# Eight slices of a modulation product multiplied and summed on VectorE instead of TensorE, with two short TensorE sums

## The chip, the core and the metric

The kernel runs on one core of a Trainium2 chip. The metric is the device time of one execution in microseconds. TensorE is called PE in the profile, VectorE DVE, ScalarE ACT, GpSimd POOL, and SyncE, which issues nearly all transfers here, SP.

## The reference, cut to what matters

The program is one layer of a hybrid backbone over 256 context and 1024 sample tokens with 1024 channels. Each of two conditioning vectors (`c_ctx` for the context tokens, `c` for the samples) gives six rows of 1024 numbers that shift, scale and gate the layer:

```python
def modulation(cond, w_ada, b_ada):
    m = jax.nn.silu(cond) @ w_ada + b_ada        # (1, 1024) @ (1024, 6144)
    return jnp.split(m[:, None, :], 6, axis=-1)   # sh1, sc1, g1, sh2, sc2, g2

h = adaln(xp, norm_mix[l], sh1, sc1)              # needed before the projection
... = project(h, ...)                             # h @ w_in, 1024 x 2848
xp = xp + g1 * merge(...)                         # g1: after the mixer
h = adaln(xp, norm_ff[l], sh2, sc2)
xp = xp + g2 * sq_relu_mlp(h, w_ff1[l], w_ff2[l])
```

Only sh1 and sc1 are needed before the projection. The other four rows, g1, sh2, sc2 and g2, are needed by later stages.

## The kernel before

**The projection stage.** `project` multiplies the normalised tokens by `w_in` in ten groups of 256 or 304 columns (`GROUPS`). A group is a row of items: ten items (one for each tile of 128 tokens) in groups 0 to 2 and 7 to 9, six items (two blocks of 128 channels by three chunks of tokens) in groups 3 to 6. `ITEMS` numbers them 0 to 83: group 1 is items 10 to 19, group 2 is 20 to 29, group 3 is 30 to 35, group 4 is 36 to 41 and group 5 begins at 42. An item is 24 matmuls (8 channel tiles, each as high*high, high*low and low*high part), written by `token_item` or `channel_item` into one of four PSUM banks; `acc_ready` counts them. All engines run through the same list of item numbers in their own programs, and each does at number `n` what the tables of numbers give it there. Each engine works strictly in the order of its program.

**What each engine does at an item.** ACT or DVE copies item `n` out of PSUM (`evacuate`; `on_act(n)` says who), and TensorE waits for that before item `n + 4`. SP stores it. Before group `g + 1` ACT splits the group's weights into a high part (L820) and POOL makes the low part (`split`, L876), which TensorE waits for at the group's first item (`wlo_ready`). SP loads the weights of a group into one of two rooms, `raw[:, 0]` and `raw[:, 1]`, in turn.

**The gates.** Beside the items runs another chain. SP loads 32 columns of the projection back (L541, in SP's program at item 12). TensorE turns them in three pieces (`Gates.pe_turn`, L572, behind items 15, 17 and 19); piece 0 waits for the load, and piece 1 and 2 each wait for `lrT_ready` of the piece before, which DVE raises with `dve_turned` (L584, at items 15, 17 and 19). DVE also makes a low part of the gate weights at item 14 (L563). From item 20 on, every seventh item has three matmuls of gate logits (L594), worked up by ACT and then by DVE in four steps (L619, L625, L631, L639 to L650).

**The modulation.** `w_ada` is used in three parts of 2048 columns; a slice is 128 of its 1024 rows by those 2048 columns, 1 MB. The first part (sh1, sc1) is done before the projection. The other sixteen slices are spread over the items of groups 2 to 9 (`slices`, `slice_at`). SP loads a slice into the room whose weights have just been split (`sp_later`, L154) and TensorE multiplies it (`pe_slice`, L198):

```python
for j in range(4):
    mm = pe.matmul(bank[32 * j:32 * j + 32, :], self.silu[:, k, :], src[:, j * HALF:(j + 1) * HALF], start=(k == 0), stop=(k == KD - 1))
```

Each of the four matmuls has the 32 columns of `silu` (two of them in use, one for each conditioning vector) as stationary operand and 512 moving columns, and writes its own 32 rows of a PSUM bank. After eight slices DVE adds the bias (`dve_rows`, L216), TensorE turns the rows into columns (`pe_turn`, L221) and DVE picks what is needed (`dve_pick`). The slices of part 1 stand behind items 23, 27, 32, 35, 38, 41, 44 and 47, those of part 2 behind items 53 to 78.

Of the kernel before, what the change touches and what calls it, by code (L numbers as in the profile page):

```python
# [20 lines left out]
P = 128  # L21
# [87 lines left out]
class Modulation:  # L109
# [5 lines left out]
    def __init__(self, s, keep, a, scratch, raw, mod_out):  # L115
# [3 lines left out]
        self.gain = s.sb("ada_gain", [P, 2, KD])  # L119
        self.gain_rows = s.sb("ada_gain_rows", [2 * KD, P])  # L120
# [22 lines left out]

    def sp_cond(self, sp):
# [7 lines left out]

    def sp_later(self, sp, m, k, j):
        sp.dma_start(self.raw_slice(j), self.source(m, k)).then_inc(self.later_in[j], 16)  # L154

    def bias(self, eng, m):
        if m:
            eng.wait_ge(self.cols_ready, m)
            if m == 2:
                eng.wait_ge(self.mod_out, 32)  # L160
        else:
            eng.wait_ge(self.cleared, 2)
        for j in range(4):
            at = (4 * m + j) * HALF
            eng.dma_start(self.rows[32 * j:32 * j + 2, :], self.a["b_ada"][:, at:at + HALF].broadcast_to([2, HALF])).then_inc(self.bias_in, 16)

# [12 lines left out]
    def dve_silu(self, dve):  # L179
        dve.memset(self.rows[:, :], 0.0).then_inc(self.cleared, 1)  # L180
        dve.memset(self.silu[:, :, :], 0.0).then_inc(self.cleared, 1)
        dve.wait_ge(self.e_ready, 1)
# [24 lines left out]
    def pe_later(self, pe, bank, m, k, j, count):  # L207
        if k == 0 and m > 1:
            pe.wait_ge(self.shift_ready, m)
        pe.wait_ge(self.later_in[j], 16 * count)  # L210
        self.pe_slice(pe, bank, self.raw_slice(j), k)

    def dve_rows(self, dve, bank, m):
        dve.wait_ge(self.slice_used, KD * (m + 1))
        dve.wait_ge(self.bias_in, 16 * 4 * (m + 1))
# [8 lines left out]
    def dve_pick(self, dve, bank, m):  # L224

        cols = bank.rearrange("p (b j r) -> p j b r", j=4, r=32)[:, :, :, 0:2]
        where = {0: ((0, 0, 0), (1, 0, 2)), 1: ((0, 1, 2),), 2: ((1, 1, 0),)}[m]
# [13 lines left out]
    def sp_store(self, sp, m):  # L241

        sp.wait_ge(self.rows_ready, m + 1)
        for j in ((0, 1) if m == 1 else (2, 3)):
# [408 lines left out]
def project(nc, keep, a, raw, hi, lo, scratch, outs, keys, rec, room, stored, mod_out):  # L653
# [4 lines left out]
    with ExitStack() as ctx:  # L658
# [26 lines left out]
        slices = [(g, at) for g, places in ((2, (3, 7)), (3, (2, 5)), (4, (2, 5)), (5, (2, 5)), (6, (5,)), (7, (2, 5, 9)), (8, (1, 5, 9)), (9, (4,))) for at in places]  # L685
        slice_at = {FIRST_ITEM[g] + at: i for i, (g, at) in enumerate(slices)}
        slice_load_at = {}
        for i, (g, at) in enumerate(slices):
            same = i and slices[i - 1][0] == g
            slice_load_at[FIRST_ITEM[g] + (slices[i - 1][1] + 1 if same else 0 if g < 7 else -1 if g == 7 else -3)] = i  # L690
        used_until = [sum(1 for g, at in slices if g <= f) for f in range(NG)]
        slice_count = [sum(1 for g, at in slices[:i + 1] if g % 2 == slices[i][0] % 2) for i in range(len(slices))]
        BANK = ps[:, 7]
        rows_at = {FIRST_ITEM[6]: 1, FIRST_ITEM[9] + 5: 2}
        cols_at = {FIRST_ITEM[6] + 1: 1, FIRST_ITEM[9] + 6: 2}
        pick_at = {FIRST_ITEM[6] + 2: 1, FIRST_ITEM[9] + 7: 2}
        assert len(slices) == 2 * KD and slices[KD - 1][0] == 5 and slices[KD] == (6, 5)

        def on_act(n):

            return n < NT or n % 2 == 1
# [19 lines left out]
        with nc.Block() as block:  # L721

            @block.sync
            def _(sp):
# [31 lines left out]
                for n in range(LAST):  # L756
# [3 lines left out]
                    if n == FIRST_ITEM[g] and 1 <= g < NG - 1:  # L760
# [4 lines left out]
                        if used_until[g - 1]:  # L765
                            sp.wait_ge(ada.slice_used, KD + used_until[g - 1])
                        load_group(sp, a, raw, g + 1, (g + 1) % 2).then_inc(w_in[(g + 1) % 2], 16)
                    if n in slice_load_at:
                        i = slice_load_at[n]
                        room = slices[i][0]  # L770
                        sp.wait_ge(wlo_ready, room)
                        sp.wait_ge(ada.slice_used, KD + (i if room == g else used_until[room - 2]))
                        ada.sp_later(sp, 1 + i // KD, i % KD, room % 2)
                    store(n)
                    if n == NT:
# [3 lines left out]
                        ada.bias(sp, 1)  # L779
# [7 lines left out]
                    if n - 1 in pick_at:  # L787
                        ada.sp_store(sp, pick_at[n - 1])
# [2546 lines left out]
```

## Time and profile before

| | |
|---|---|
| time, median of 3 runs | 1642.98 us (1642.93 to 1643.2) |
| the profiled execution, its own time | 1642.75 us |
| span of its instructions | 1641.0 us |
| PE busy | 1587.1 us (97%) |
| DVE, POOL, ACT busy | 977.2, 1018.1, 687.4 us |
| projection stage on PE, from item 10 to the end | about 83 to 388 us |

The span runs from the first to the last instruction; the execution's own time is 1.8 us more. A busy share counts instructions under way, so the share of an engine says where it has idle time and not how well it works. Times of rows are microseconds from the span's start.

### The profile page before, as it was taken

To read this page: it belongs to the slowest core of one execution; us is meant where nothing else is said; L and a number is where in the kernel's file an instruction comes from. 1 tells how busy PE (TensorE), PEld (TensorE's weight loads), DVE (VectorE), ACT (ScalarE), POOL (GpSimd) and SP (SyncE) were. 2 spreads that over 40 slices of the span, in tenths; PEclk is the share of its full clock that TensorE was granted. 3 is DMA by queue.
4 is the path that set the end of the run, shared out by engine and by line. 5 is a ranking of instruction groups with operands and counts; after the bars stand their busy time and mean duration, and the time that the engine had idled before them with its cause. 6 is when DMAs were issued, how large, how long until landed. Compare 5 with 4: busy or idle time off the path is not lost.

```text
span 1641.0 us, 31942 instructions
## 1 busy us (share of the span) xinstructions
PE 1587.1 (97%) x11619; PEld 1388.8 (85%) x11619; DVE 977.2 (60%) x1503; ACT 687.4 (42%) x1213; POOL 1018.1 (62%) x784
## 2 busy tenths in 40 slices
PE   5999999998999999999899999999999999999998
PEld 1998778997788877788789899898979899998987
DVE  2733564775665575347865756666684545545468
ACT  2513323324454666213444444444545444444441
POOL 1711455573585899004687778677898767677673
PEclk9999999999999999999999999999999999999999
DMA  9254655749745654334643132231344132231313
GB/s 345 89 146 151 199 177 192 259 141 248 225 161 178 213 175 136 132 133 154 209 164 103 51 102 77 76 102 51 103 140 143 52 102 79 75 102 51 102 52 116
DMA packets 209402, 225.93 MB, mean 138 GB/s; under 512 B 50688, under 2 KB 169616, under 8 KB 206096
## 3 DMA queue, kind: packets, MB, share of 16 engines
q1 hardware_dynamic: 209248, 224.46, 43.1%
q8 instruction: 70, 1.15, 0.3%
q14 instruction: 36, 0.29, 0.1%
q10 hardware_dynamic: 48, 0.02, 0.0%
HBM read 177.22 MB, written 47.24 MB: 137 GB/s over the span
## 4 chain that ended last, share of the span: by engine, by line
PE 44%; POOL 4%; DVE 1%; issue 1%; DMA 0%; ACT 0%; SPq 0%; DVEq 0%; ACTq 0%; POOLq 0%
PE ff_banks L3200 8%; PE ff_banks L3201 8%; PE ff_banks L3202 8%; PE ff_banks L3173 7%; PE ff_banks L3175 7%; PE ff_banks L3174 7%; POOL h_whi L2846 1%; POOL h_xop L2443 1%; POOL h_wlo L2858 1%; POOL h_whi L2853 1%; DVE ff_tmp L3047 0%; DMA ff_hb<-in_w_ff 0%; DVE ff_acc L3037 0%; PE ff_banks L3215 0%; PE ff_banks L3216 0%
## 5 line engine op out<-in xcount | busy, mean ns | idle before, releaser
L3173 PE MATMUL ff_banks<-h_xop,h_whi 128*128 128x320 f32 x888 | 275.2, 310 | 4.6 <-POOL h_whi L2846 2.0
L3175 PE MATMUL ff_banks<-h_xop,h_whi 128*128 128x320 f32 x888 | 274.4, 309 | 0.0
L3174 PE MATMUL ff_banks<-h_xop,h_whi 128*128 128x320 f32 x888 | 274.3, 309 | 0.0
L3004 DVE TENSOR_TENSOR ff_acc<-ff_acc,ff_banks 128x512 f32<-128x512 f32 x296 | 200.4, 681 | 100.7 <-PE ff_banks L3202 99.1
L3200 PE MATMUL ff_banks<-h_wlo 128*128 128x512 f32 x580 | 226.5, 390 | 1.6 <-POOL h_whi L2853 0.8
L3202 PE MATMUL ff_banks<-h_wlo 128*128 128x512 f32 x580 | 225.6, 389 | 0.0
L2846 POOL TENSOR_TENSOR h_whi<-mid_raw,h_whi 128x512 fp32r<-128x512 f32 x149 | 208.5, 1415 | 1.4 <-ACT h_whi L2698 1.4
L2858 POOL TENSOR_TENSOR h_wlo<-mid_raw,h_wlo 128x320 fp32r<-128x320 f32 x128 | 116.8, 914 | 127.3 <-ACT mid_raw L2735 127.3
L3173 PEld LDWEIGHTS ff_banks<-h_xop,h_whi 128*128 128x128 f32 x888 | 166.7, 188 | 8.3 <-issue 3.6
L3174 PEld LDWEIGHTS ff_banks<-h_xop,h_whi 128*128 128x128 f32 x888 | 166.7, 188 | 1.1
L3175 PEld LDWEIGHTS ff_banks<-h_xop,h_whi 128*128 128x128 f32 x888 | 166.7, 188 | 0.0
L981 PE MATMUL prj_banks<-prj_whi,h_hi 128*128 128x304 f32 x480 | 147.6, 308 | 5.1 <-POOL h_lo L351 2.9
L2846 POOL TENSOR_TENSOR h_whi<-ff_tmp,h_whi 128x512 fp32r<-128x512 f32 x63 | 105.6, 1676 | 67.7 <-ACT h_whi L2698 67.7
L983 PE MATMUL prj_banks<-prj_whi,h_lo 128*128 128x304 f32 x480 | 144.9, 302 | 0.0
L982 PE MATMUL prj_banks<-prj_wlo,h_hi 128*128 128x304 f32 x480 | 144.3, 301 | 0.0
L2698 ACT ACTIVATE h_whi<-mid_raw 128x512 fp32r<-128x512 f32 x149 | 90.0, 623 | 97.7 <-DVE mid_raw L2960 91.4
L3200 PEld LDWEIGHTS ff_banks<-h_wlo 128*128 128x128 f32 x580 | 108.9, 188 | 25.0 <-DVE ff_acc L3004 1.9
L3202 PEld LDWEIGHTS ff_banks<-h_wlo 128*128 128x128 f32 x580 | 108.9, 188 | 22.9
L2728 ACT ACTIVATE mid_raw<-wo_raw 128x320 f32<-128x320 f32 x128 | 60.3, 471 | 159.4 <-DVE wo_raw L2982 65.2
L3201 PE MATMUL ff_banks<-h_whi,h_wlo 128*128 128x512 f32 x310 | 120.7, 390 | 0.0
L831 ACT ACTIVATE prj_stage<-prj_banks 128x304 f32<-128x304 f32 (+2 forms) x47 | 21.0, 447 | 221.2 <-PE prj_banks L983 134.4
L3201 PE MATMUL ff_banks<-h_wlo 128*128 128x512 f32 x290 | 113.1, 390 | 0.0
(326 smaller groups left out, 3771.2 us busy)
## 6 DMA issues: line engine op xcount, KB each, us to landing
mid_raw<-in_w_ff SPq DMA_DIRECT2D x124, 512.0 KB, 4.4
mid_raw<-in_w_ada SPq DMA_DIRECT2D x18, 1024.0 KB, 7.0
early_room<-qk_by_channel SPq DMA_DIRECT2D x20, 512.0 KB, 4.1
proj<-prj_stage SPq DMA_DIRECT2D x60, 152.0 KB, 1.9
mid_raw<-in_w_in SPq DMA_DIRECT2D x6, 1216.0 KB, 7.7
early_room<-in_w_ada SPq DMA_DIRECT2D x6, 1024.0 KB, 10.4
decays<-early_room SPq DMA_DIRECT2D x8, 640.0 KB, 4.5
early_room<-decays SPq DMA_DIRECT2D x20, 256.0 KB, 2.8
```

The lines of the kernel that those rows point to most:

```text
L981: pe.matmul(out, x_hi, whi[j][:, k, 0:w], start=(k == 0), stop=False)
L982: pe.matmul(out, x_hi, wlo[j][:, k, 0:w], start=False, stop=False)
L983: mm = pe.matmul(out, x_lo, whi[j][:, k, 0:w], start=False, stop=(k == KD - 1))
L2846: pool.tensor_tensor(lo, source(q, i), hi.bitcast(F32), ALU.subtract).then_inc(w1lo_ready, 1)
L2858: pool.tensor_tensor(ulo[j][c][:, t0:t0 + TH], v[i % 2], uhi[j][c][:, t0:t0 + TH].bitcast(F32), ALU.subtract).then_inc(ulo_ready, 1)
L3004: dve.tensor_tensor(acc[:, p, at], acc[:, p, at], down[n % RING], ALU.add).then_inc(added, 1)
L3173: pe.matmul(out, w_hi[:, k], x_hi[:, k], start=(k == 0), stop=False)
L3174: pe.matmul(out, w_hi[:, k], x_lo[:, k], start=False, stop=False)
L3175: mm = pe.matmul(out, w_lo[:, k], x_hi[:, k], start=False, stop=(k == KH - 1))
L3200: pe.matmul(out, x_hi, w_hi[c][:, at], start=(c == 0), stop=False)
L3201: pe.matmul(out, x_hi, w_lo[c][:, at], start=False, stop=False)
L3202: mm = pe.matmul(out, x_lo, w_hi[c][:, at], start=False, stop=(c == 1))
```

## The change

The eight slices of part 1 (g1 and sh2) leave TensorE. They are loaded in another cut: 256 rows of `w_ada` by 1024 columns, again 1 MB, first the four loads of g1 (`u = 0`) and then the four of sh2 (`u = 1`). DVE multiplies each row by its number of `silu` and adds up over the channel tiles in `sums`, four instructions of 128x1024 for each load. What then is left, the sum over the 128 partitions, TensorE makes with four matmuls for each `u`, whose stationary operand `pick` is a column of ones (`pe_sum`). The loads begin in group 1 instead of group 2. The bias rows, the stores of g1 and the turn of sh2 move with it, and ACT evacuates all items below 36, where DVE took the even ones from 10 on. A parameter of the build makes a reserved piece of on-chip memory smaller; `sums` is a new tensor there.

```diff
+    def sp_early(self, sp, i, j):
+        u, q = i // 4, i % 4
+        src = self.a["w_ada"][0, 2 * q * P:(2 * q + 2) * P, self.quarter(u):self.quarter(u) + 2 * HALF]
+        sp.dma_start(self.raw_slice(j).rearrange("p (k n) -> p k n", k=2), src.rearrange("(k p) n -> p k n", p=P)).then_inc(self.later_in[j], 16)
...
+    def dve_early(self, dve, i, k, j, count):
+        u, q = i // 4, i % 4
+        dve.wait_ge(self.later_in[j], 16 * count)
+        for c in range(2):
+            t = 4 * i + 2 * k + c
+            by = self.silu[:, 2 * q + k, c:c + 1]
+            in_ = self.raw_slice(j)[:, 2 * k * HALF:(2 * k + 2) * HALF]
+            if t % 16 < 2:
+                if u:
+                    dve.wait_ge(self.sum_ready, u)
+                op = dve.tensor_scalar(self.sums[:, c], in_, by, None, ALU.mult)
+            else:
+                dve.wait_ge(self.product_ready, t - 1)
+                op = dve.scalar_tensor_tensor(self.sums[:, c], in_, by, self.sums[:, c], ALU.mult, ALU.add)
+            op.then_inc(self.product_ready, 1)
+
+    def pe_sum(self, pe, bank, u):
+        pe.wait_ge(self.picked, 3)
+        pe.wait_ge(self.product_ready, 16 * (u + 1))
+        if u:
+            pe.wait_ge(self.rows_ready, u + 1)
+        for c, j, row, at in self.places(u):
+            mm = pe.matmul(bank[row - c:row - c + 32, :], self.pick[:, c], self.sums[:, c, j * HALF:(j + 1) * HALF], start=True, stop=True)
+        mm.then_inc(self.sum_ready, 1)
...
-        slices = [(g, at) for g, places in ((2, (3, 7)), (3, (2, 5)), (4, (2, 5)), (5, (2, 5)), (6, (5,)), (7, (2, 5, 9)), (8, (1, 5, 9)), (9, (4,))) for at in places]
+        early = ((1, 0, 1, 1), (1, 2, 3, 3), (1, 4, 5, 5), (2, 0, 1, 2), (2, 3, 4, 5), (2, 6, 7, 8), (3, 0, 1, 2), (3, 3, 4, 5))
+        late = ((6, 5), (7, 2), (7, 5), (7, 9), (8, 1), (8, 5), (8, 9), (9, 4))
...
+        sum_at = {FIRST_ITEM[2] + 4: 0, FIRST_ITEM[4] + 1: 1}
+        early_rows_at = {n + 1: u for n, u in sum_at.items()}
+        shift_turn, shift_at = FIRST_ITEM[4] + 3, FIRST_ITEM[4] + 4
...
-            return n < NT or n % 2 == 1
+            return n < FIRST_ITEM[4] or n % 2 == 1
...
+                    if n in early_load_at:
+                        i = early_load_at[n]
+                        room = early[i][0]
+                        sp.wait_ge(wlo_ready, room)
+                        before = i if i and early[i - 1][0] == room else early_until[room - 2] if room > 1 else 0
+                        if before:
+                            sp.wait_ge(ada.product_ready, 4 * before)
+                        ada.sp_early(sp, i, room % 2)
...
-    nc = bacc.Bacc("TRN2", target_bir_lowering=False, num_devices=1)
+    nc = bacc.Bacc("TRN2", target_bir_lowering=False, num_devices=1, dynamic_dma_scratch_size=1024)
```

An entry of `early` is the group whose room is used, the item of that group at which SP loads, and the two items at which DVE multiplies the first and the second half. The loads are called 0 to 7 below.

On DVE, group 1 read before, from the first copy out of PSUM to the third piece of the turned columns:

```order
L913 COPY prj_stage<-prj_banks 128x304 x2
L563 TENSOR_TENSOR prj_wgk<-early_room,prj_wgk 32x1024
L584 TENSOR_TENSOR prj_lrT<-prj_banks,prj_lrT 32x512
L913 COPY prj_stage<-prj_banks 128x304
L584 TENSOR_TENSOR prj_lrT<-prj_banks,prj_lrT 32x512
L913 COPY prj_stage<-prj_banks 128x304
L584 TENSOR_TENSOR prj_lrT<-prj_banks,prj_lrT 32x256
```

and now, in the changed kernel's line numbers (L634 is L563 of before, L655 is L584):

```order
L250 TENSOR_SCALAR prj_ada_sums<-mid_raw,prj_ada_silu 128x1024 x2
L253 SCALAR_TENSOR_TENSOR prj_ada_sums<-mid_raw,prj_ada_silu,prj_ada_sums 128x1024 x6
L634 TENSOR_TENSOR prj_wgk<-early_room,prj_wgk 32x1024
L655 TENSOR_TENSOR prj_lrT<-prj_banks,prj_lrT 32x512
L253 SCALAR_TENSOR_TENSOR prj_ada_sums<-mid_raw,prj_ada_silu,prj_ada_sums 128x1024 x4
L655 TENSOR_TENSOR prj_lrT<-prj_banks,prj_lrT 32x512
L655 TENSOR_TENSOR prj_lrT<-prj_banks,prj_lrT 32x256
```

Eight products now stand ahead of the gate weights and piece 0, and four more between piece 0 and piece 1; the copies are gone to ACT.

On SP, the same stretch read before, from the gate weights' bias to the weights of group 3:

```order
L165 DMA prj_ada_rows<-in_b_ada 2x512 x4
L735 DMA proj<-prj_stage 128x304 x2
L541 DMA early_room<-proj 128x10x32 x3
L735 DMA proj<-prj_stage 128x304 x7
L387 DMA mid_raw<-in_w_in 128x8x256
```

and now (L812 is the store of an item, L612 the load of the gates' columns, L458 the load of a group's weights, L167 one of the new loads):

```order
L187 DMA prj_ada_rows<-in_b_ada 1x512 x4
L812 DMA proj<-prj_stage 128x304
L167 DMA mid_raw<-in_w_ada 128x2x1024
L812 DMA proj<-prj_stage 128x304
L612 DMA early_room<-proj 128x10x32 x3
L812 DMA proj<-prj_stage 128x304
L167 DMA mid_raw<-in_w_ada 128x2x1024
L812 DMA proj<-prj_stage 128x304 x6
L458 DMA mid_raw<-in_w_in 128x8x256
```

Loads 1 and 2 have moved into this stretch (load 0 stands further ahead, at item 10), and load 1 stands in front of the gates' columns. All three use room 1, so each waits until the products of the one before are done.

## Rows read from the trace of the kernel before

**Rows 1.** The page: busy time and share of each engine.

```profile
PE 1587.1 (97%) x11619; PEld 1388.8 (85%) x11619; DVE 977.2 (60%) x1503; ACT 687.4 (42%) x1213; POOL 1018.1 (62%) x784
```

**Rows 2.** Busy time by stretch: PE, PEld, DVE, ACT, POOL, clock, DMA share, GB/s.

```profile
83.00:388.00 305.00, 303.24 (x1940) 269.29 (x1938) 158.79 (x170) 88.47 (x106) 125.56 (x78) 1.00 0.59 187
```

**Rows 3.** Waits of PE from 83 to 388: total, times, longest.

```profile
PE prj_banks L198 <- DMA mid_raw<-in_w_ada: 0.5, 1, 0.5
```

**Rows 4.** Timeline, items 23 to 25 leaving PSUM, a slice behind 23.

```profile
130.56 0.42 ACT L831 ACTIVATE prj_stage<-prj_banks 128x304 f32<-128x304 f32 x1 [0.84 <-PE prj_banks L983]
135.08 0.47 DVE L913 COPY prj_stage<-prj_banks 128x304 f32<-128x304 f32 x1 [5.55 <-PE prj_banks L983]
138.42 0.43 ACT L831 ACTIVATE prj_stage<-prj_banks 128x304 f32<-128x304 f32 x1 [5.63 <-PE prj_banks L983]
```

**Rows 5.** DVE line 296: ns min/median/max.

```profile
L296 DVE TENSOR_SCALAR head_x<-head_x,head_rstd x10: 735/753/1645, 24.8 to 66.2; 128x1024 f32<-128x1024 f32 x10
```

**Rows 6.** DVE by form: total and mean ns of one.

```profile
L1409 DVE TENSOR_TENSOR early_at<-mix_gla,keep_mats 128x1024 f32<-128x1024 f32 x20 | 24.4, 1221 | 2.1 <-PE mix_gla L1297 1.5
L488 DVE SCALAR_TENSOR_TENSOR prj_xn<-early_room,prj_rstd 128x640 f32<-128x640 f32 x10 | 8.2, 816 | 1.8 <-POOL prj_rstd L462 1.8
```

**Rows 7.** Timeline of SP's queue, group 1.

```profile
82.94 0.43 SPq L387 DMA_DIRECT2D mid_raw<-in_w_in  x1
...
93.52 0.83 SPq L735 DMA_DIRECT2D proj<-prj_stage  x2
94.53 2.08 SPq L541 DMA_DIRECT2D early_room<-proj  x3
```

**Rows 8.** Landing of the slice issued at 117.76, behind a group's weights.

```profile
DMA to landing us min/median/max: 7.8/7.8/7.8
```

**Rows 9.** Landing of the slice issued at 131.65, alone.

```profile
DMA to landing us min/median/max: 5.2/5.2/5.2
```

**Rows 10.** Landing of the gates' columns, L541, three loads.

```profile
DMA to landing us min/median/max: 2.7/3.8/3.9
```

**Rows 11.** Timeline of PE, turned pieces 0, 1, 2 of the gates.

```profile
101.96 0.60 PE L572 MATMUL prj_banks<-keep_mats,early_room 128*96 128x128 f32 x4
...
109.09 0.60 PE L572 MATMUL prj_banks<-keep_mats,early_room 128*96 128x128 f32 x4
...
116.20 0.38 PE L572 MATMUL prj_banks<-keep_mats,early_room 128*96 128x128 f32 x2
```

**Rows 12.** Timeline of POOL and DVE, group 1.

```profile
99.05 5.41 POOL L876 TENSOR_TENSOR prj_wlo<-mid_raw,prj_whi 128x2432 fp32r<-128x2432 f32 x1 [17.94 <-ACT prj_whi L820]
...
99.33 6.21 DVE L563 TENSOR_TENSOR prj_wgk<-early_room,prj_wgk 32x1024 fp32r<-32x1024 f32 x1
```

**Rows 13.** Timeline of DVE, pieces 0 and 1.

```profile
105.57 0.68 DVE L584 TENSOR_TENSOR prj_lrT<-prj_banks,prj_lrT 32x512 fp32r<-32x512 f32 x1
...
110.35 0.68 DVE L584 TENSOR_TENSOR prj_lrT<-prj_banks,prj_lrT 32x512 fp32r<-32x512 f32 x1 [3.59 <-ACT prj_lrT L578]
```

**Rows 14.** Timeline of DVE, POOL and ACT, group 4.

```profile
195.97 1.91 ACT L820 ACTIVATE prj_whi<-mid_raw 128x2048 fp32r<-128x2048 f32 x1
...
198.28 0.42 DVE L911 TENSOR_SCALAR prj_stage<-prj_banks 128x256 f32<-128x256 f32 x1 [5.24 <-PE prj_banks L993]
...
207.89 4.61 POOL L876 TENSOR_TENSOR prj_wlo<-mid_raw,prj_whi 128x2048 fp32r<-128x2048 f32 x1
```

**Rows 15.** Timeline of PE, end of group 4 (item 41).

```profile
213.20 0.75 PE L594 MATMUL prj_banks<-prj_lrT,prj_wgk 96*128 96x512 f32 x3
213.88 1.07 PE L198 MATMUL prj_banks<-mid_raw,prj_ada_silu 128*32 128x512 f32 x8
```

**Rows 16.** Timeline of PE and DVE, rows of part 1.

```profile
251.57 0.68 DVE L216 TENSOR_TENSOR prj_ada_rows<-prj_banks,prj_ada_rows 128x512 f32<-128x512 f32 x1
...
256.89 0.60 PE L221 MATMUL prj_banks<-keep_mats,prj_ada_rows 128*128 128x128 f32 x4
```

**Rows 17.** Landing of all sixteen slices, L154.

```profile
DMA to landing us min/median/max: 5.1/6.7/10.0
```

More of the change, by code:

```diff
@@ new lines, in pe_sum, with dve_early_rows @@
+    def pe_sum(self, pe, bank, u):
+        pe.wait_ge(self.picked, 3)
+        pe.wait_ge(self.product_ready, 16 * (u + 1))
+        if u:
+            pe.wait_ge(self.rows_ready, u + 1)
+        for c, j, row, at in self.places(u):
+            mm = pe.matmul(bank[row - c:row - c + 32, :], self.pick[:, c], self.sums[:, c, j * HALF:(j + 1) * HALF], start=True, stop=True)
+        mm.then_inc(self.sum_ready, 1)
+    def dve_early_rows(self, dve, bank, u):
+        dve.wait_ge(self.sum_ready, u + 1)
+        dve.wait_ge(self.bias_in, 16 * 4 * (u + 2))
+        dve.tensor_tensor(self.rows[:, :], bank, self.rows[:, :], ALU.add).then_inc(self.rows_ready, 1)
@@ new lines, in dve_shift, with sp_early_store @@
+    def dve_shift(self, dve, bank):
+        cols = bank.rearrange("p (b j r) -> p j b r", j=4, r=32)
+        dve.wait_ge(self.cols_ready, 2)
+        for c in range(2):
+            dve.tensor_copy(self.keep["shift"][:, 1].rearrange("p (j b) c -> p j b c", j=2)[:, :, :, c], cols[:, 2 * c:2 * c + 2, :, c]
+                            ).then_inc(self.shift_ready, 1)
+    def sp_early_store(self, sp):
+        sp.wait_ge(self.rows_ready, 2)
+        for c, j, row, at in self.places(0):
+            sp.dma_start(self.scratch["mod"][c:c + 1, at:at + HALF], self.rows[row:row + 1, :]).then_inc(self.mod_out, 16)
@@ new lines, in project @@
+        late = ((6, 5), (7, 2), (7, 5), (7, 9), (8, 1), (8, 5), (8, 9), (9, 4))
+        early_load_at = {FIRST_ITEM[g] + load: i for i, (g, load, a0, a1) in enumerate(early)}
+        early_at = [(FIRST_ITEM[g] + at, i, k) for i, (g, load, a0, a1) in enumerate(early) for k, at in enumerate((a0, a1))]
+        slice_at = {FIRST_ITEM[g] + at: i for i, (g, at) in enumerate(late)}
+        slice_load_at = {}
+        for i, (g, at) in enumerate(late):
+            same = i and late[i - 1][0] == g
+            slice_load_at[FIRST_ITEM[g] + (late[i - 1][1] + 1 if same else 0 if g < 7 else -1 if g == 7 else -3)] = i
@@ new lines, in project @@
+        early_until = [sum(1 for e in early if e[0] <= f) for f in range(NG)]
+        late_until = [sum(1 for e in late if e[0] <= f) for f in range(NG)]
+        slices = [e[0] for e in early + late]
+        slice_count = [sum(1 for g in slices[:i + 1] if g % 2 == slices[i] % 2) for i in range(len(slices))]
+        BANK = ps[:, 7]
+        sum_at = {FIRST_ITEM[2] + 4: 0, FIRST_ITEM[4] + 1: 1}
+        early_rows_at = {n + 1: u for n, u in sum_at.items()}
+        shift_turn, shift_at = FIRST_ITEM[4] + 3, FIRST_ITEM[4] + 4
@@ L699, in on_act @@
+        rows_at, cols_at, pick_at = FIRST_ITEM[9] + 5, FIRST_ITEM[9] + 6, FIRST_ITEM[9] + 7
+        assert len(early) == KD and len(late) == KD
         def on_act(n):
-            return n < NT or n % 2 == 1
+            return n < FIRST_ITEM[4] or n % 2 == 1
         def staged_value(n):
```

101 lines of the change are left out of this document (61 added, 40 removed).

## The prediction

> **What bounds the kernel now.** I read the page first: TensorE is busy 97% of the span, the other engines 42 to 62% [rows 1]. The reader sees that work taken from TensorE can shorten the kernel, and that the others have room on the average. The change lies in the projection stage, so I read its stretch next. TensorE is busy 303.24 of 305 us there, DVE 158.79, POOL 125.56, ACT 88.47, at full clock and with transfers at 0.59 of their time [rows 2]. Last I read what TensorE waits for there: one wait of 0.5 us, for a slice [rows 3]. So in this stage each microsecond of matmuls taken away counts in full, until TensorE starts to wait for something that today is ready just in time. The task is to find that.
>
> **What leaves TensorE.** Item 24 leaves PSUM 4.52 us after item 23, with a slice between them, and item 25 leaves 3.34 us after 24, without one [rows 4]. A slice thus costs 1.18 us of TensorE. Eight are removed, -9.4 us. Two sums of four matmuls are added; they have the shape of a slice (128 rows deep, 32 stationary and 512 moving columns), so I price them the same, +2.4. The turn of sh2 moves from item 49 to 39 and costs what it did. Net -7.1 us if nothing waits.
>
> **What DVE gets.** 32 instructions of 128x1024 in fp32. The four that open a sum scale one tensor, as line 296 does, 0.75 us [rows 5]. The other 28 have two tensors. A 128x1024 with one input in PSUM takes 1.22, and the same operation on 640 columns takes 0.82, of which 384 further columns at the same pace make 1.22 too [rows 6]. Some of it overlaps, so four take about 4.7. Together some 36 us over 100 us in which DVE is half idle, and it gives the copies of 13 items to ACT, which has the most room. The work fits; what counts is when each piece is done, because DVE, SP and TensorE take their programs in order.
>
> **The chain of loads in group 1.** Loads 0, 1 and 2 use one room, so each waits for the products of the one before.
> Load 0 is issued behind the weights of group 2, at 83.4 [rows 7]. A slice issued so landed after 7.8 us [rows 8]: 91.2. Two single and two double products, 3.9: 95.1.
> Load 1 is issued at 95.1. SP would have come there at about 94.2, so the store of item 12 and the gates' columns are issued some 1.6 us later than today's 94.53 [rows 7]. Load 1 alone takes 5.2 [rows 9]: 100.3.
> **Piece 0.** Today the gates' columns are issued by 96.6, the last landing 3.9 after its start near 95.7 [rows 7, 10], 99.6, and TensorE wants them at 101.96 [rows 11]: 2.4 to spare. Now they are 1.6 later and behind 1 MB, for which the queued slice paid 7.8 - 5.2 = 2.6 [rows 8, 9]. They land at 103.8, and TensorE waits 1.8.
> **Pieces 1 and 2.** When load 1 lands at 100.3, POOL is in its low part of group 2's weights, 99.05 to 104.46, and the DVE instruction with two on-chip inputs that began beside it took 6.21 us for what alone is some 1.2: it ended 1.08 after POOL did [rows 12]. I take the products to wait likewise (the nearest row; there is none of exactly this operation beside POOL). Then load 1's products run 104.5 to 109.2; the gate weights (1.2) and piece 0 (0.68, [rows 13]) make 111.1, 2 us after piece 1 is wanted at 109.09 [rows 11]. Load 2 is issued at 109.2, lands at 114.4, its products end at 119.1, and piece 1 of DVE, which stands behind them, at 119.8. TensorE wants it for piece 2 at 116.20 [rows 11]: 3.6 late, with hand-overs 4.0. The three waits are one delay after another on the same engine, so the largest counts, not the sum: +4.0.
> The bounds of this term: if the products don't wait for POOL, load 1's end at 105.0, load 2's at 114.9 and piece 1 at 115.6, in time; then piece 0's 1.8 is left. If also the columns land in time, 0. If load 2 lands after 7.8 instead of 5.2, +6.6.
>
> The Trainium skill, in "SBUF — State Buffer", section "Who interferes with whom", says that a VectorE instruction with two SBUF inputs and a GpSimd instruction that reads SBUF exclude each other for the whole instruction. It speaks of tensor_tensor. The trace agrees for that operation [rows 12]; for the three-operand product no run here shows it. By the rule the sum is the one above; without it 2.2 us less.
>
> **After group 1.** The chain goes on at about 12 us a load (issue to landing 5.2 to 7.8, products 4.7). Load 3 is issued with group 3's weights when load 2's products end, lands near 127, and its products end near 132. The first sum stands behind item 24, which leaves PSUM at 135.08 - 1.18 + 4.0 = 137.9 [rows 4]. Loads 4 to 7 then end near 146, 157, 171 and 187, also held back by gate work, by POOL's low parts and by the wait of SP for its item. The second sum stands behind item 37, some 3 us before item 38's 198.28 [rows 14]. So the sums have 5 to 8 us to spare. The group weights that now wait for products are tightest for group 5: issued at 187, landed by 193, and ACT splits them at 195.97 today [rows 14]. Under that cover all this costs nothing; without it each microsecond is one of TensorE's.
> **Group 5's weights.** Today POOL's low part for group 5 ends at 212.50, 14.2 after DVE copied item 38 at 198.28 [rows 14]. Between them stands a chain that starts with that copy. DVE now also adds the bias of the second sum there, 0.68 [rows 16]: 14.9. TensorE ends item 41 at 213.20 [rows 15], 14.9 after; less a slice (1.18), plus the turn (0.60 busy, some 0.4 of time, [rows 16]) and the gate logits (0.68, [rows 15]) it wants the weights at 14.8. The two are level: +0.2, bounds 0 and 1. Today's slack of 2.4 us (the slice at 213.88 takes about 1, [rows 15]) is gone, and what is later on DVE in group 4 is late on TensorE.
> Behind group 5 nothing is added to DVE, and the splits of groups 6 to 9 follow the copies of items, which come earlier with TensorE. The mixer's loads are issued behind the last items and move with them.
>
> **The sum.** -7.1 + 4.0 + 0.2 = -2.9 us. The profiled execution took 1642.75, so 1639.9; the median of the runs is 0.23 above it: 1640.1.
>
> **The rivals.**
> A, forecast: TensorE gains 7.1 and waits 3 to 5 us in group 1; -1.9 to -4.1, 1638.9 to 1641.1. Chance 0.55.
> B, the wait is small: the products pass POOL, or the columns and load 2 land early. For it speaks that no row shows this operation waiting; against it, that its nearest kin does [rows 12]. -4.9 with the wait for piece 0, -7.1 with none: 1635.9 to 1638.1. Chance 0.22.
> C, longer: transfers of the new cut land after 6.5 to 7.8, or POOL starts late behind weights that load 0 pushed back (it delays the gates' weights by up to 2.6, and ACT splits group 2 behind them). Then piece 1 is 6 to 8 late: net -1 to +1, 1642 to 1644. Chance 0.13.
> D, slower: slices of today land after up to 10.0 us [rows 17]. At 10.0 each of seven later loads is 4.8 behind my chain. Load 2 alone makes the wait 8.8, net +1.9. From where the five loads behind it add more than the 5 to 8 us to spare, the second sum waits as well, 5 x 4.8 = 24 less the 8 and less what TensorE has been held up already (9): +7 on top, +9, 1652. It decides from some 1.5 us a load. Against it: in today's order only stores of items stand in the queue between the gates' columns and group 3's weights, and the slice that was alone took 5.2 [rows 9]. Chance 0.10.
>
> **How the numbers follow.** A measurement of this kernel tells 0.2%, 3.3 us, from no change: faster is under 1639.7, slower over 1646.3. B is all faster, and of A about 0.35 of its 0.55, since its middle lies 0.4 us above the line: faster 0.22 + 0.21 = 0.43 with C adding none. D is slower for the larger part, 0.09, and C near none. Same is the rest, 0.48. The range takes A, most of B and C: 1636.0 to 1644.0, which leaves out D and a tenth besides. A's own range is 1638.9 to 1641.1.
>
> **What would show it.** In the profile after: slices behind eight items fewer and two sums; TensorE waiting for DVE line 655 (the third turned piece) 3 to 5 us near 116 to 120, and for the gates' columns near 102; a product of load 1 with a duration of about 5 us beside POOL's low part; no wait at the two sums; group 5's first matmul within a microsecond of POOL's end. The prediction is wrong if TensorE doesn't wait near 120, if it waits at a sum, or if the stage is shorter but the mixer gives it back, which would be seen as longer idle of TensorE behind its start.

## The result, and the profile after

The changed kernel takes 1649.03 us (median of 10 runs, 1646.59 to 1654.32), the one before 1643.15 (10 runs, 1642.64 to 1644.43): a ratio of 1.0038 (1.003 to 1.0046). It is 5.9 us slower where 2.9 faster was forecast. The profiled execution took 1649.0, and its page reads

```profile
span 1647.2 us, 31905 instructions
...
PE 1584.2 (96%) x11571; PEld 1391.1 (84%) x11571; DVE 1009.9 (61%) x1527; ACT 693.4 (42%) x1226; POOL 1017.1 (62%) x784
```

TensorE has 48 matmuls less (eight slices fewer and two sums more, each shown as x8) and is busy 2.9 us less [rows 1], yet the span is 6.2 us longer: its idle time has grown by 9. The view of waits, PE from 60 to 395 us (in total, times, longest), says at whose hands:

```profile
PE prj_banks L643 <- DVE prj_lrT L655: 4.5, 2, 2.8
PE prj_banks L643 <- DMA early_room<-proj: 2.6, 1, 2.6
PE mix_st L1597 <- PEq L95: 2.3, 1, 2.3
PE prj_banks L224 <- DMA mid_raw<-in_w_ada: 1.3, 1, 1.3
PE prj_banks L1089 <- POOL prj_wlo L967: 0.9, 1, 0.9
```

L643 is the turning of the gates' columns (L572 before), L655 the DVE step behind each piece, L224 a slice that stayed, L1089 the first matmul of group 5. Before, the stage had only the slice's wait, at 0.5 [rows 3]. The third row is at the start of the mixer, the stage behind the projection; the kernel before has 2.2 us there as well. The timeline of PE, all three turned pieces:

```profile
103.23 0.64 PE L643 MATMUL prj_banks<-keep_mats,early_room 128*96 128x128 f32 x4 [2.58 <-DMA early_room<-proj]
...
112.19 0.64 PE L643 MATMUL prj_banks<-keep_mats,early_room 128*96 128x128 f32 x4 [1.62 <-DVE prj_lrT L655]
...
122.36 0.67 PE L643 MATMUL prj_banks<-keep_mats,early_room 128*96 128x128 f32 x2 [2.85 <-DVE prj_lrT L655]
```

They stood at 101.96, 109.09 and 116.20 without a wait [rows 11]. Who made DVE late is in its timeline and POOL's:

```profile
90.21 1.42 DVE L250 TENSOR_SCALAR prj_ada_sums<-mid_raw,prj_ada_silu 128x1024 f32<-128x1024 f32 x2 [10.59 <-DMA mid_raw<-in_w_ada]
91.54 2.48 DVE L253 SCALAR_TENSOR_TENSOR prj_ada_sums<-mid_raw,prj_ada_silu,prj_ada_sums 128x1024 f32<-128x1024 f32 x2
100.10 10.07 DVE L253 SCALAR_TENSOR_TENSOR prj_ada_sums<-mid_raw,prj_ada_silu,prj_ada_sums 128x1024 f32<-128x1024 f32 x4 [6.09 <-DMA mid_raw<-in_w_ada]
110.20 1.22 DVE L634 TENSOR_TENSOR prj_wgk<-early_room,prj_wgk 32x1024 fp32r<-32x1024 f32 x1
111.45 0.68 DVE L655 TENSOR_TENSOR prj_lrT<-prj_banks,prj_lrT 32x512 fp32r<-32x512 f32 x1
116.72 4.87 DVE L253 SCALAR_TENSOR_TENSOR prj_ada_sums<-mid_raw,prj_ada_silu,prj_ada_sums 128x1024 f32<-128x1024 f32 x4 [4.58 <-DMA mid_raw<-in_w_ada]
121.62 0.68 DVE L655 TENSOR_TENSOR prj_lrT<-prj_banks,prj_lrT 32x512 fp32r<-32x512 f32 x1
```

```profile
100.14 5.36 POOL L967 TENSOR_TENSOR prj_wlo<-mid_raw,prj_whi 128x2432 fp32r<-128x2432 f32 x1 [20.47 <-ACT prj_whi L911]
```

Four products take 4.87 alone (load 2's, at 116.72) and 10.07 beside POOL's 5.36 (load 1's): 5.2 us more, about the length of POOL's instruction. The gates' columns are late in SP's queue:

```profile
94.10 0.39 SPq L167 DMA_DIRECT2D mid_raw<-in_w_ada  x1
94.54 1.04 SPq L812 DMA_DIRECT2D proj<-prj_stage  x1
95.75 4.93 SPq L612 DMA_DIRECT2D early_room<-proj  x3
...
110.24 0.37 SPq L167 DMA_DIRECT2D mid_raw<-in_w_ada  x1
```

The three loads of the columns (L612) start 1.2 us later than L541 did and take 4.93 us to issue instead of 2.08 [rows 7]. Last, what the waits did to the clock. The windows view (PE, PEld, DVE, ACT, POOL, clock, DMA share, GB/s) of an undisturbed stretch, of the third wait and of what follows it:

```profile
103.20:106.60 3.40, 3.37 (x25) 3.37 (x26) 3.40 (x2) 0.60 (x1) 2.30 (x1) 1.00 0.00 0
120.00:122.30 2.30, 0.00 (x0) 0.00 (x0) 2.27 (x3) 0.00 (x0) 0.00 (x0) 1.00 0.20 68
122.30:125.70 3.40, 3.34 (x14) 3.33 (x15) 0.42 (x2) 0.38 (x1) 0.00 (x0) 0.50 0.83 257
```

For 3.4 us behind the wait TensorE ran at 1.2 GHz instead of 2.4 and began 14 matmuls, not 25: 11 of 0.14 us, 1.5 us lost.

**Where the time went, by stretch.** I measure with the copies of items out of PSUM. Before, items 9, 20 and 83:

```profile
82.12 0.42 ACT L831 ACTIVATE prj_stage<-prj_banks 128x304 f32<-128x304 f32 x1 [2.91 <-PE prj_banks L983]
...
119.96 0.47 DVE L913 COPY prj_stage<-prj_banks 128x304 f32<-128x304 f32 x1 [2.41 <-PE prj_banks L983]
...
386.73 0.42 ACT L831 ACTIVATE prj_stage<-prj_banks 128x304 f32<-128x304 f32 x1 [4.54 <-PE prj_banks L983]
```

and in the changed kernel:

```profile
80.65 0.42 ACT L922 ACTIVATE prj_stage<-prj_banks 128x304 f32<-128x304 f32 x1 [2.91 <-PE prj_banks L1081]
...
127.68 0.42 ACT L922 ACTIVATE prj_stage<-prj_banks 128x304 f32<-128x304 f32 x1 [4.24 <-PE prj_banks L1081]
...
389.32 0.42 ACT L922 ACTIVATE prj_stage<-prj_banks 128x304 f32<-128x304 f32 x1 [4.54 <-PE prj_banks L1081]
```

Up to item 9 the changed kernel is 1.5 us ahead. The start differs from profile to profile (six of the twelve below are ahead by 1.3 to 1.6 us, the others by 0.1 to 0.5), and nothing of the change stands there. Item 9 to 20 takes 47.03 instead of 37.84, +9.2. Item 9 to 83, "the stage" from here on, takes 308.67 instead of 304.61: +4.1, where -2.9 was forecast. From there to the end it loses another 3.7.

### The profile page after: what moved, and what is told of

Same layout as the page of the kernel before. It is cut to its first block, busy times and chain, and to the rows that moved or that the text cites. A ratio compares the mean times of both kernels' runs of the same rounds, so it can differ in the third digit from the quotient of the medians.

```text
span 1647.2 us, 31905 instructions
## 1 busy us (share of the span) xinstructions
PE 1584.2 (96%) x11571; PEld 1391.1 (84%) x11571; DVE 1009.9 (61%) x1527; ACT 693.4 (42%) x1226; POOL 1017.1 (62%) x784
## 4 chain that ended last, share of the span: by engine, by line
PE 44%; POOL 4%; DVE 1%; issue 1%; DMA 0%; ACT 0%; DVEq 0%; POOLq 0%; ACTq 0%; SPq 0%
PE ff_banks L3302 8%; PE ff_banks L3303 8%; PE ff_banks L3304 8%; PE ff_banks L3275 7%; PE ff_banks L3276 7%; PE ff_banks L3277 7%; POOL h_whi L2948 1%; POOL h_xop L2545 1%; POOL h_wlo L2960 1%; POOL h_whi L2955 1%; DVE ff_tmp L3149 0%; DMA ff_hb<-in_w_ff 0%; POOL h_wlo L2955 0%; DVE ff_acc L3139 0%; DVE ff_acc L3106 0%
## 5 line engine op out<-in xcount | busy, mean ns | idle before, releaser
L922 ACT ACTIVATE prj_stage<-prj_banks 128x304 f32<-128x304 f32 (+2 forms) x60 | 26.8, 446 | 206.2 <-PE prj_banks L1081 128.8
```

## The experiments

All in one table first: the stage of each profile against before's 304.61 us, the median, and the ratio to the kernel before on record, with its 95% interval. The ratio is taken to executions of the kernel before that were timed beside the run (their medians lie between 1642.7 and 1643.7 us), and it isn't the quotient of two medians. The stage comes from one profiled execution of each kernel. For e3 and e12 that execution took 4.4 and 5.3 us more than the kernel's median (1648.08 and 1651.27), so their stages are likely longer than usual; for the others that were timed it lies within 2 us of the median.

| kernel | stage, us | median, us | ratio to before |
|---|---|---|---|
| the change | +4.1 | 1649.03 | 1.0038 (1.003 to 1.0046) |
| e1_memory | +0.3 | 1641.94 | 1.0003 (0.9994 to 1.0012) |
| e2_copies | 0.0 | 1643.64 | 1.0001 (0.9992 to 1.001) |
| e3_pool_later | +1.5 | 1643.64 | 1.001 (0.9999 to 1.002) |
| e4_order | +0.9 | 1645.32 | 1.0014 (1.0004 to 1.0023) |
| e5_tiny | +0.1 | 1643.02 | 0.9998 (0.9989 to 1.0008) |
| e6_order_all | +4.5 | 1650.05 | 1.004 (1.0026 to 1.0053) |
| e7_order_sum | +8.1 | 1653.85 | 1.0065 (1.0051 to 1.0079) |
| e8_seven_gone | -5.5 | 1636.8 | 0.9963 (0.9949 to 0.9976) |
| e9_both | -2.5 | 1644.01 | 1.0006 (0.9997 to 1.0016) |
| e10_semaphores | 0.0 | one profile | |
| e11_load_behind | +2.4 | one profile | |
| e12_group3 | +0.8 | 1645.95 | 1.0022 (1.0012 to 1.0033) |

The theory: the slices are worth what was said, and the chain load, product, shared room, next load is what makes TensorE wait in group 1. The rivals: the smaller reserved memory and the new tensors, the copies that went to ACT, or a gain that the mixer gives back.

**e1_memory** is the kernel before with the build parameter and the two new tensors, unused.

```diff
+        self.sums = s.sb("ada_sums", [P, 2, 2 * HALF])
+        self.pick = s.sb("ada_pick", [P, 2, 32])
...
+    nc = bacc.Bacc("TRN2", target_bir_lowering=False, num_devices=1, dynamic_dma_scratch_size=1024)
```

> The kernel before with only the smaller reserve of on-chip memory and the two new tensors allocated, not used. Chain theory (the time was lost in the projection stage, by waits of TensorE on DVE in group 1 and what follows): same as before, within 0.5 us. Layout theory (of the 6 us, the 3.7 that the profile after shows behind the projection stage come from other memory addresses): 2 to 4 us slower than before, all of it behind 390 us.

**e2_copies** adds to it that ACT copies all items below 36.

```diff
-            return n < NT or n % 2 == 1
+            return n < FIRST_ITEM[4] or n % 2 == 1
```

> As the first, and ACT copies all items below 36 out of PSUM, where DVE took the even ones. No load, product or slice is moved. Chain theory: same as before, within 1 us, as ACT is half idle and TensorE needs an item's bank only three items later. Copies theory (ACT behind gate work and behind stores is what TensorE waited for): TensorE waits for ACT in groups 1 to 3, 2 us or more slower.

Neither moves the stage or the median. Both rivals fall.

**e8_seven_gone** is the kernel before with seven of part 1's eight slices cut to 8 of 512 columns; it leaves out most of g1 and sh2. It shows what TensorE could gain if nothing ever waited.

```diff
+            mm = pe.matmul(bank[32 * j:32 * j + 32, 0:w], self.silu[:, k, :], src[:, j * HALF:j * HALF + w], start=(k == 0), stop=(k == KD - 1))
...
+        self.pe_slice(pe, bank, self.raw_slice(j), k, 8 if m == 1 and k else HALF)
```

> The kernel before, with the slices of part 1 after the first cut to 8 of their 512 columns on TensorE (g1 and sh2 come out other than the reference's), nothing given to DVE. Price theory (a slice costs 1.18 us of TensorE and nothing is behind it): 7 slices less, but their weight loads of 0.1 us stay, 5 to 8 us shorter at the end of the stage, and 5 to 8 us faster in all. Rival (what the projection stage gains, the start of the mixer gives back in idle time or clock): shorter by that much at the end of the stage, but less than 3 us faster in all.

The stage is 5.5 us shorter, 0.79 at each cut slice, and the median of the whole kernel 6.1. So matmuls taken out of this stage count in full to the end. The one profile does lose 2.1 us at the mixer's start, but so do profiles of e2 and e10 (3.1 and 3.4), where nothing was taken out, and the medians show no loss. That rival falls too, for a kernel with the old chain.

**e5_tiny** is the changed kernel with products of 8 columns instead of 1024; it leaves out nearly all of g1 and sh2. Loads, rooms, waits and sums stay.

```diff
-                op = dve.scalar_tensor_tensor(self.sums[:, c], in_, by, self.sums[:, c], ALU.mult, ALU.add)
+                op = dve.scalar_tensor_tensor(self.sums[:, c, 0:8], in_[:, 0:8], by, self.sums[:, c, 0:8], ALU.mult, ALU.add)
```

> The changed kernel with every product on DVE cut from 1024 to 8 columns (g1 and sh2 come out other than the reference's; the loads, waits and sums are all there). Chain theory: a chain of loads of 6.2 us and products of 4.9 to 10 became late; with products of 0.3 it is 17 us shorter by load 2, so the third turned piece has no wait, but the gates' columns still stand behind load 1 and TensorE waits some 2 to 4 us for them. Stage about 8 to 9 us shorter than the changed kernel's. Rival (transfers alone, not DVE, hold the stage up): at most 3 us shorter.

Pieces 1 and 2 wait no more; only the columns do, on PE (L644 is L643):

```profile
103.87 1.09 PE L644 MATMUL prj_banks<-keep_mats,early_room 128*96 128x128 f32 x4 [3.27 <-DMA early_room<-proj]
```

```profile
102.70:109.50 6.80, 5.63 (x23) 5.61 (x24) 4.87 (x6) 0.59 (x1) 2.47 (x1) 0.50 0.53 125
```

The clock was halved for 6.8 us around and behind it, and item 19 is 6.04 late: 3.3 us of waiting and 2.8 of clock. So the products cost 4.0 of the stage, less than the 8 to 9 expected, since one wait for the crowded queue costs 6 by itself; the change has a cost even when the products take next to nothing.

**e3_pool_later** is the changed kernel with POOL's low part of group 2's weights behind load 1's products.

```diff
+                    if g == 2:
+                        pool.wait_ge(ada.product_ready, 8)
```

> The changed kernel, with one wait more: POOL makes the low part of group 2's weights only when the products of load 1 are done. Exclusion theory (the products of load 1 took 10.07 us instead of 4.9 since POOL's low part lay in them for 5.4): the four products take 4.9 us from 100.1, load 2 is issued near 105, the third turned piece is wanted and ready within 1 us of each other, 4 to 6 us faster than the changed kernel. Rival (the products are slow by themselves or by the transfers): the products still take about 10 us and the time is that of the changed kernel.

Load 1's products on DVE take what load 2's do:

```profile
102.06 4.87 DVE L253 SCALAR_TENSOR_TENSOR prj_ada_sums<-mid_raw,prj_ada_silu,prj_ada_sums 128x1024 f32<-128x1024 f32 x4 [6.80 <-DMA mid_raw<-in_w_ada]
```

So the extra 5.2 us came from POOL's low part beside them. The waits at pieces 1 and 2 are gone. The columns' wait stayed, and here, at 3.3 us, there was halved clock around its end, +6.2 at item 17 where the changed kernel, with 2.6 and no halved clock, had +2.8. The profiled execution is one of three of this kernel at 1648 to 1649 us; the other seven took 1642.1 to 1645.8. Whether they had the halved clock no trace shows.

**e11_load_behind** is the changed kernel with load 1 issued at item 13, behind the columns.

```diff
-        early = ((1, 0, 1, 1), (1, 2, 3, 3), (1, 4, 5, 5), ...
+        early = ((1, 0, 1, 1), (1, 3, 3, 3), (1, 4, 5, 5), ...
```

> The changed kernel with load 1 issued one item later, behind the gates' columns, its products where they were. Queue theory: TensorE's wait of 2.6 us for the columns goes (piece 0), but load 1 lands 2 to 3 us later, its products still end behind POOL's low part and the waits at pieces 1 and 2 are what they were or longer: the stage 0 to 2 us shorter than the changed kernel's. Rival (the load in front of the columns is the root of all three waits): stage 6 us or more shorter.

```profile
113.12 1.09 PE L643 MATMUL prj_banks<-keep_mats,early_room 128*96 128x128 f32 x4 [4.00 <-DVE prj_lrT L655]
```

The columns' wait is gone: it was the 1 MB in front of them. The lateness comes back one piece later, 4.0 us with halved clock around its end, since load 1's products start 5 us later (105.19). The stage is 1.6 us shorter than the changed kernel's, as expected.

**e4_order** also moves the multiplying: load 1 is issued at item 13 and multiplied at 15, load 2 at 16 and 17.

```diff
-        early = ((1, 0, 1, 1), (1, 2, 3, 3), (1, 4, 5, 5), ...
+        early = ((1, 0, 1, 1), (1, 3, 5, 5), (1, 6, 7, 7), ...
```

> The changed kernel with only the places of loads 1 and 2 in group 1 changed: load 1 is issued at item 13 (behind the gates' columns instead of in front) and multiplied at item 15 (behind the gate weights and turned piece 0), load 2 is issued at item 16 and multiplied at item 17, behind turned piece 1. Order theory (what TensorE waited for was small gate work queued behind the products): no wait at pieces 0 and 1, at most 1 us at piece 2, 7 to 9 us faster than the changed kernel, 1 to 3 us faster than before. Rival (the added DVE work and the transfers themselves make the stage longer, wherever they stand): within 2 us of the changed kernel.

```profile
122.60 0.81 PE L665 MATMUL prj_banks<-prj_lrT,prj_wgk 96*128 96x512 f32 x3 [3.81 <-DVE prj_lrT L655]
```

No piece is waited for, but the first gate logits (L665, L594 before) are, behind piece 2's DVE step, which stands behind load 2's products. 3.8 us of waiting and 3.4 us at half clock make most of the 5.8 us by which item 21 is late. The stage is 3.2 us shorter than the changed kernel's, where 7 to 9 was expected.

**e6_order_all** multiplies load 2 at item 19, behind piece 2's step.

```diff
-(1, 6, 7, 7)
+(1, 6, 9, 9)
```

> Like the run with the order changed, but load 2 is multiplied at item 19, behind the last turned piece, so that no gate work of group 1 stands behind a product that waits. Order theory: no wait at the three pieces nor at the first gate logits (3.8 us there in the run before, with 1.7 of a halved clock behind it), the stage 5 to 6 us shorter than in that run and 4 to 6 shorter than before the change. Rival: as products end 2 to 4 us later, TensorE waits at the first sum or for group 3's weights instead, and the stage gains less than 2.

Group 1 has no wait left (item 20 is where it was before). The first sum has it, on PE, with DVE and POOL ahead of it:

```profile
141.08 1.93 PE L262 MATMUL prj_banks<-prj_ada_sums,prj_ada_pick 128*32 128x512 f32 x8 [7.68 <-DVE prj_ada_sums L253]
```

```profile
131.82 9.12 DVE L253 SCALAR_TENSOR_TENSOR prj_ada_sums<-mid_raw,prj_ada_silu,prj_ada_sums 128x1024 f32<-128x1024 f32 x4 [9.83 <-DMA mid_raw<-in_w_ada]
...
132.41 5.05 POOL L967 TENSOR_TENSOR prj_wlo<-mid_raw,prj_whi 128x2048 fp32r<-128x2048 f32 x1 [26.62 <-ACT prj_whi L911]
```

Again products beside POOL, now beside group 3's low part. The wait of 7.7 us is 10.7 of lateness; the 6.8 us at half clock began 3.1 us before the wait ended. This is what the rival of the expectation said, and the stage is longer than before's, not 4 to 6 shorter.

**e7_order_sum** puts the second sum two items later, behind item 39, to relieve group 5.

```diff
-        sum_at = {FIRST_ITEM[2] + 4: 0, FIRST_ITEM[4] + 1: 1}
+        sum_at = {FIRST_ITEM[2] + 4: 0, FIRST_ITEM[4] + 3: 1}
```

> The same, and the second sum stands behind item 39 instead of 37, its bias on DVE at item 40 and its turn behind item 41, all behind the DVE work that feeds POOL's low part of group 5's weights. Theory of the tail (the bias and DVE's delay stand ahead of that chain): the 1 us that TensorE waits for POOL at group 5 goes, another 0.5 to 1 us faster. Rival (the wait has to do with when DVE comes there at all, not with the bias): same as the run without it, within 0.3 us in the stage.

TensorE's wait for POOL at group 5 went, and the turn of sh2 waited 2.9 us for DVE's bias instead, again with halved clock behind it: the stage is 3.6 us longer than e6's, which neither expectation had.

**e9_both** is e6 with POOL's low parts of groups 3 and 4 behind the products of loads 3 and 6, and the first sum one item later.

```diff
-        sum_at = {FIRST_ITEM[2] + 4: 0, FIRST_ITEM[4] + 1: 1}
+        sum_at = {FIRST_ITEM[2] + 5: 0, FIRST_ITEM[4] + 1: 1}
...
+                    if g in (3, 4):
+                        pool.wait_ge(ada.product_ready, {3: 16, 4: 28}[g])
```

> The order of the run in which load 2 stands behind the last turned piece, and what that run's trace asks for: POOL makes the low parts of groups 3 and 4 only when the products of loads 3 and 6 are done, and the first sum stands behind item 25 instead of 24. Theory (what is left is the exclusion of DVE and POOL, 4.2 us in the products of load 3 there, and a sum that comes 3 us too early): no wait in groups 1 to 4 over 1 us, the stage 4 to 6 us shorter than before the change, 2 to 5 us faster in all. Rival (each repair moves the wait on, since DVE's chain has no slack left): a wait of 2 us or more at a sum, at POOL's low part of group 3 or 4, with a halved clock behind it, and no faster than before.

Its waits, PE from 60 to 395:

```profile
PE prj_banks L1091 <- POOL prj_wlo L969: 3.4, 2, 2.3
PE mix_st L1599 <- PEq L95: 2.3, 1, 2.3
PE prj_banks L224 <- DMA mid_raw<-in_w_ada: 1.0, 1, 1.0
```

Nothing waits for DVE, and no wait in the stage reaches 2.5 us or is followed by halved clock. The stage is 6.5 us shorter than the changed kernel's and 2.5 shorter than before's (4 to 6 was expected). POOL is waited for at group 4's start, 1.1 us, the price of holding it back, and at group 5's, 2.3. As a whole the kernel is level with before, where 2 to 5 us faster was expected.

**e12_group3** takes that wait of POOL in group 4 away again.

```diff
-                    if g in (3, 4):
-                        pool.wait_ge(ada.product_ready, {3: 16, 4: 28}[g])
+                    if g == 3:
+                        pool.wait_ge(ada.product_ready, 16)
```

> The kernel of the last order with the two waits of POOL, but without the wait of group 4's low part (POOL waits for the products of load 3 alone, in group 3). In that kernel POOL began group 4's low part at 174.53, behind the products of load 6 (28), next to a scan of DVE, and took 7.05 us; TensorE waited 2.3 us for it at group 4's first item and 1.1 at group 5's. Theory (the added wait of POOL, not the exclusion, costs the start of group 4): POOL begins near 168.2, where ACT's split ends, and is done by 175, 4 us before TensorE wants it; the products of load 6 beside it get up to 5 us later and the second sum still has that to spare. TensorE waits for nothing over 1 us but group 5's weights, the stage is 4.5 to 5.5 us shorter than before's, and the median 1640.5 to 1643, level with before or up to 0.15% below it because kernels with the new products lose 1.6 to 2.3 us behind the stage. Rival: the products of loads 6 and 7 slip by the 5 us each and the second sum waits 3 us or more; then the clock is halved after it and the stage is no shorter than before's, 1645 to 1647.

Two stretches of its timeline, all engines:

```profile
168.68 4.62 POOL L969 TENSOR_TENSOR prj_wlo<-mid_raw,prj_whi 128x2048 fp32r<-128x2048 f32 x1 [26.91 <-ACT prj_whi L911]
168.79 7.79 DVE L253 SCALAR_TENSOR_TENSOR prj_ada_sums<-mid_raw,prj_ada_silu,prj_ada_sums 128x1024 f32<-128x1024 f32 x2 [7.01 <-DMA mid_raw<-in_w_ada]
...
215.24 0.80 PE L1091 MATMUL prj_banks<-h_hi,prj_whi 128*128 128x512 f32 x1 [4.09 <-POOL prj_wlo L969]
```

The first expectation missed (it also had e9's two waits swapped). The rival had the time and the halved clock right, but not the place. Group 4 starts in time and the second sum doesn't wait. But two products took 7.79 instead of the 2.48 they take alone, DVE is 1.0 us later through group 4, and so is POOL's low part for group 5 (210.68 against e9's 209.65), while TensorE comes there 0.8 us earlier. The wait of 2.3 grew to 4.1, and 6.8 us of halved clock lie around its end: the stage is 3.2 us longer than e9's. That profile is of the slowest of the eight executions, though: by the ratios to before e12 is 2.6 us slower than e9, and their intervals overlap a little.

**e10_semaphores** adds to e1 the three new semaphores, unused, for the time lost behind the stage.

```diff
+        self.picked, self.product_ready, self.sum_ready = (s.sem("ada_" + n) for n in ("picked", "product_ready", "sum_ready"))
```

> The run with the memory layout alone, and the three new semaphores allocated, not used. Asks where the 1.5 to 2.1 us come from that all kernels with the new products lose between 440 us and the end, and the kernels made from the one before don't (0.2). Semaphore theory: this run loses 1 us or more there. Rival (it comes with what the new kernels do in the stage or store for the later ones): 0.4 or less.

Between 440 us and the end its one profile loses 0.3 us on before, where the changed kernel loses 2.0. The semaphores are not the cause.

## Why the prediction was wrong

The step that failed is the term for the wait in group 1: +4.0 us in the sum, +9.2 in the trace. Two smaller steps failed beside it: group 5's weights (+0.2, measured +1.2), and the statement that what stands behind the stage moves with it, where another 3.7 us were lost. The misses are 5.2, 1.0 and 3.7 us. With 0.8 in small steps at late slices, less the 1.5 by which this profile started early, they make about the 9.1 us between the 1639.9 forecast and the 1649.0 measured.

**The slices and the sums: right.** Each removed slice moved the items behind it by -1.19, each sum by +1.18, and no sum waited. Products: 4.87 for four, forecast 4.7.

**The wait in group 1: the term that failed.** Forecast +4.0, measured +9.2. Its mechanism stood: load 1's products were excluded by POOL, the last of three waits decided, and it was the third turned piece, at DVE L655. What was mis-sized, in its parts:

- The chain was 3.7 us later, counted from item 9: piece 2 began 41.7 us after it (122.36 - 80.65), forecast 38.1 (120.2 - 82.12). About 2.5 of it is POOL: its low part began 19.5 us after item 9 instead of 16.9, because the gate weights landed behind load 0 and ACT waited 2.45 us for them, to 96.88. The other 1.2 is load 2, which landed after 6.4 us and not the 5.2 of [rows 9]: my price was that of a load alone in the queue, while [rows 17] had a median of 6.7. Both were named, in rival C, and given 0.13.
- The clock, 1.5 us. It was in neither the sum nor any bound. In the runs it is the larger surprise: a wait of 3.3 cost 6.0 and 6.2 (e5, e3), one of 3.8 cost 5.6 (e4), one of 7.7 cost 10.7 (e6).

4.0 + 3.7 + 1.5 is 9.2. The columns' wait, forecast 1.8, was 2.6: I had priced their landing and not their issue, 4.93 us instead of 2.08. In the changed kernel that hid in the later wait; e3's profile shows that, alone, it can cost 6.2.

**"The largest counts, not the sum".** True of pieces that lag one chain (the waits sum to 7.05, and with the clock's 1.5 to 8.6 of the 9.2; the last piece alone fixes the total), but it hid that taking one wait away brings up the next: e3, e11, e4, e6, e7 and e12 each removed a wait, and each time another was left or came in its place; against the kernel each was made from (e6 from e4, e7 from e6, e12 from e9, the others from the changed one), the stage became between 3.7 us longer and 3.2 shorter.

**The exclusion: right.** The product, scalar_tensor_tensor with two inputs in SBUF, is longer by about POOL's whole instruction: 10.07 beside POOL's 5.36, 9.12 beside 5.05 (e6, where the first product began 0.6 us before POOL), 4.87 with POOL held back (e3). The rule of the Trainium skill ("SBUF — State Buffer", section "Who interferes with whom"), that a VectorE instruction with two SBUF inputs and a GpSimd one that reads SBUF exclude each other, names only tensor_tensor as an example; these rows agree with it for a second operation.

**Group 5.** Forecast 0.2 with a bound of 1; the wait was 0.93 and the lateness 1.2. Another 0.8 us went in steps of less than 0.4 at late slices and item 61, which no term had. With these, 9.2 - 7.1 + 1.2 + 0.8 is the 4.1 of the stage.

**Behind the stage: located, its cause not tested.** I said that the mixer moves with the items. The medians of e8 bear that out, but the changed kernel's profile lost 3.7 us there. About 1.6 of it lies at the mixer's start, 385 to 440 us. The profiles of all kernels have a stretch or two of halved clock there, of 3.4 to 13.7 us (before one of 3.4, the changed kernel two), and they lose between 0.2 and 5.6 us against before, e2's and e10's 3.1 and 3.4 without any of the new products. So one profile can't say what the change costs there.

The other 2.0 lie between 440 and the end: all nine kernels with the new products lose 1.6 to 2.3 there against before, and the four others 0.4 at most. It isn't the memory, the copies or the semaphores (e1, e2, e10), nor the length of the products (e5, 1.6). Most of it comes in two steps, about 0.8 and 0.6 us in the changed kernel. One is near 680 us: the load of the gate g1 (`mrg_gate`) lands after 5.5 to 6.1 us instead of 3.9 to 4.1, the load behind it after 6.4 to 6.9 instead of 4.8 to 5.0, and TensorE waits 0.3 to 0.8 us for that one. The view of transfers shows the two loads before and in the changed kernel, and a transfer of another queue beside the latter:

```profile
mrg_gate<-mod_rows SPq DMA_DIRECT2D x1, 512.0 KB, 3.9
mid_raw<-mix SPq DMA_DIRECT2D x1, 512.0 KB, 4.8
...
q8 instruction: 1, 0.02, 1.2%
mrg_gate<-mod_rows SPq DMA_DIRECT2D x1, 512.0 KB, 5.9
mid_raw<-mix SPq DMA_DIRECT2D x1, 512.0 KB, 6.8
```

The other step is near 1225 us, where a load of feed-forward weights lands after 5.0 to 5.6 us instead of 4.0 to 4.3. In all nine kernels a packet of the queue named instruction (16 KB, 0.9 to 1.8 us long) stands beside the first pair of loads and one or two beside the second; in the five others there is none at either place. The nine have fewer instructions on TensorE and more on DVE and SP than before; e1 and e10 have the same, and e2 moves 26 from DVE to ACT. So the packets may stand elsewhere because the programs have another length. No run moves a packet by itself: that they are the cause is likely, and not shown. This loss is a good part of why e9, 2.5 shorter in the stage, is not faster in all; its profile lost another 2.5 at the mixer's start.

**The chances.** Rival D had the sign, by longer transfers that make a sum wait; no load took 10 us (5.8 to 8.2, median 6.4) and no sum waited, so it came right for another reason in the changed kernel, though e6 made its wait at a sum. I had given slower 0.09 by adding up only lateness; a stall of some 3 us, which I thought probable, had a second price.

## What to carry to other kernels

Work taken from an engine at 97% is worth its full time only if every chain that the receiving engines serve keeps its slack: walk each small step that the busy engine waits for (here 0.68 us of DVE) and ask what multi-microsecond work now stands in front of it in its queue. Behind each predicted TensorE wait of some 3 us count the halved clock as well, which cost 1.5 to 3 us where it could be told apart here. Price a load from rows with the queue as full as it will be, and price its issue, not only its landing.

## What the runs showed of the hardware

- In the projection stage each of the nine TensorE waits of 2.85 to 7.7 us came with 3.4 or 6.8 us at 1.2 GHz, which began between 3.1 us before the wait's end and 1.3 us behind it; waits of 1.1, 1.6, 2.3 and 2.6 us came without. The length alone doesn't decide: the wait of 2.3 us at the mixer's start had 1.2 GHz within 1.2 us behind it in six profiles (the changed kernel's at 392.0 us) and not in the kernel before.
- scalar_tensor_tensor on 128x1024 in fp32 from SBUF takes 1.22 us in a row of four (4.87), and two or four of them together take 4.3 to 5.4 us more beside one POOL tensor_tensor of 4.6 to 5.4.
- Three small loads took 4.93 us to issue with a 1 MB load issued 1.6 us ahead of them, and 5.46 and 5.50 in e5 and e3, against 2.08 to 3.41 in the kernels without (2.08 before, 3.41 in e4 and e12).
- Two loads of 512 KB landed some 1.4 to 2.2 us later in each of the nine profiles that had a 16 KB instruction packet beside them (near 680 us) than in the five that had none.
- A slice of four matmuls with 32 stationary and 512 moving columns costs 1.18 us; with 8 moving columns it still costs 0.39.
